# The down projection starts its seven-product blocks one quadruple earlier, loads one weight sum by itself, and moves some background sums

## The reference

```python
h = rms_norm(x, attn_norm);  p = h @ w_in            # 2048 -> 5376
mix = concat(sliding_window_attention(...), hgrn2(...))
x = x + mix @ w_out                                  # 2048 -> 2048
h = rms_norm(x, ffn_norm)
u = causal_conv3(h @ w_up) + conv_b                  # 2048 -> 2 x 5632
a, b = split(u)
x = x + (silu(a) * b) @ w_down                       # 5632 -> 2048
```

## Time and profile before

| | us |
|---|---|
| median of 3 runs | 1083.93 |
| the profiled execution | 1085.06 |
| its span | 1083.2 |
| PE busy | 1074.6 (99%) |
| DVE busy | 907.2 (84%) |
| ACT busy | 638.1 (59%) |
| POOL busy | 87.5 (8%) |

### The profile page before, as it was taken

The page is one execution under the profiler, slowest core; times in us unless marked ns, Lnnn a source line. Parts: engine busy times, 40 slices in busy tenths (PEclk is TensorE's granted clock), DMA queues, the critical chain, the costliest instruction groups (busy, mean ns, idle before and its releaser), DMA issues.

```text
span 1083.2 us, 18131 instructions
## 1 busy us (share of the span) xinstructions
PE 1074.6 (99%) x6537; PEld 925.9 (85%) x6537; DVE 907.2 (84%) x1342; ACT 638.1 (59%) x934; POOL 87.5 (8%) x130
## 2 busy tenths in 40 slices
PE   9999999999999999999999999999999999999998
PEld 8888888888888888888888888888888887787887
DVE  7888988979655578888888889888887888998998
ACT  7677675757445555555555555545554566657763
POOL 4500000000010010100100010001010000000000
PEclk9999999999999999999999999999999999999999
DMA  8656679787799988988988988989988689989794
GB/s 277 180 170 193 182 234 243 228 242 225 255 246 281 274 249 251 260 259 254 262 240 257 265 253 265 250 238 293 280 253 236 196 296 308 326 295 340 269 339 154
DMA packets 197008, 274.00 MB, mean 253 GB/s; under 512 B 9285, under 2 KB 144086, under 8 KB 196694
## 3 DMA queue, kind: packets, MB, share of 16 engines
q1 hardware_dynamic: 180758, 220.69, 62.4%
q0 software_dynamic: 12960, 47.19, 20.0%
q10 hardware_dynamic: 3232, 5.39, 1.3%
HBM read 267.86 MB, written 52.56 MB: 296 GB/s over the span
## 4 chain that ended last, share of the span: by engine, by line
PE 95%; DMA 3%; DVE 1%; issue 0%; ACT 0%; SPq 0%; DVEq 0%; ACTq 0%
PE bank L1828 38%; PE bank L1836 20%; PE bank L2221 6%; PE bank L2223 6%; PE bank L2222 6%; PE bank L2074 3%; PE bank L2075 3%; PE bank L2076 3%; PE bank L1875 2%; PE bank L1877 2%; PE bank L1876 2%; DMA slot<-u_sums 1%; PE bank L1796 1%; PE bank L1904 1%; DMA raw<-in_w_ffn_up_dram 1%; DMA xt<-in_x_dram 1%
## 5 line engine op out<-in xcount | busy, mean ns | idle before, releaser
L796 ACT CAST w_hi<-raw 128x1024 fp32r<-128x1024 f32 x299 | 312.3, 1049 | 245.9 <-PE bank L1836 107.3
L1209 DVE TENSOR_TENSOR w_lo<-raw,w_hi 128x1024 fp32r<-128x1024 f32 x299 | 364.0, 1222 | 107.2 <-ACT w_hi L796 106.5
L1828 PE MATMUL bank<-hs,w_hi 128*128 128x512 f32 x1792 | 423.0, 391 | 0.0
L1828 PEld LDWEIGHTS bank<-hs,w_hi 128*128 128x128 f32 x1792 | 331.2, 188 | 66.3 <-issue 0.9
L1836 PEld LDWEIGHTS bank<-hs,w_lo 128*128 128x128 f32 x1792 | 224.6, 191 | 5.7 <-issue 0.2
L1836 PE MATMUL bank<-hs,w_lo 128*128 128x256 f32 x1792 | 227.3, 283 | 0.0
L1175 ACT CAST hi_slot<-slot 128x1024 fp32r<-128x1024 f32 (+1 forms) x108 | 124.3, 1187 | 65.4 <-PE bank L2223 19.1
L1736 DVE TENSOR_TENSOR slot_lo<-slot,hi_slot 128x1536 fp32r<-128x1536 f32 (+1 forms) x74 | 142.1, 1957 | 3.6 <-ACT hi_slot L1175 2.4
L1654 DVE SCALAR_TENSOR_TENSOR C<-U,cols,C 128x256 f32<-128x256 f32 x176 | 73.4, 479 | 0.0
L2223 PE MATMUL bank<-hi_slot,gated 128*128 128x512 f32 (+1 forms) x186 | 72.0, 387 | 0.0
L2221 PE MATMUL bank<-hi_slot,gated 128*128 128x512 f32 (+1 forms) x186 | 72.0, 387 | 0.0
(11 more groups left out here) (249 smaller groups left out, 1191.2 us busy)
## 6 DMA issues: line engine op xcount, KB each, us to landing
raw<-in_w_ffn_up_dram SPq DMA_DIRECT2D x176, 512.0 KB, 5.7
u_sums<-in_w_ffn_down_dram POOLq DMA_DIRECT2D x62, 512.0 KB, 6.1
raw<-in_w_in_dram SPq DMA_DIRECT2D x51, 512.0 KB, 4.5
slot<-in_w_ffn_down_dram SPq DMA_DIRECT2D x40, 512.0 KB, 5.0
raw<-in_w_in_dram SPq DMA_DIRECT2D x66, 256.0 KB, 3.6
slot<-u_sums SPq DMA_DIRECT2D x22, 768.0 KB, 5.9
raw<-in_w_out_dram SPq DMA_DIRECT2D x32, 512.0 KB, 5.8
u_sums<-u_sums POOLq DMA_DIRECT2D x28, 512.0 KB, 7.2
```

What stands on the lines that cost most here:

```text
L796: act.copy(w_hi[:, i, :], raw[:, i, :]).then_inc(units_hi, 1)
L1209: dve.tensor_tensor(w_lo[:, i, :], raw[:, i, :], w_hi[:, i, :].bitcast(F32), ALU.subtract)\
L1828: m = pe.matmul(banks[b][:, :], w_hi[:, i, c], hs[:, 4 * i + k, :], start=(first and k == 0), stop=(final and k == 3))
```

## The change

- The first pair's pattern has three plain quadruples in the old ring in place of four, then eight sevens, a plain quadruple D in the small slot, nine sevens and a last plain one. The counts, 17 sevens and 5 plain ones, are as before. With three old quadruples the last up group splits six pieces, not eight, and which old piece frees which block is worked out by `last_old_in`.
- The fourth sum, where it lies in DRAM, has a load and a semaphore of its own; the two others are loaded when part y of the slot's last use is done.
- POOL's steps come every 8/3 units, not 14/5, and none waits for a unit from 110 to 119.

The diff, without the two `b_work` functions' inner lines (they skip the split of units 2 and 3 where a quadruple has only two) and the new semaphore's line:

```diff
@@ -79,7 +79,7 @@
 COLUMN_PAIRS = OUT_GROUPS // 2
-PATTERNS = ["CCCCSSSSSSSSSSSSSSSSSc", "CcSSSSSSSDSSSSSSSSSSCc"]
+PATTERNS = ["CCCSSSSSSSSDSSSSSSSSSc", "CcSSSSSSSDSSSSSSSSSSCc"]
 KINDS = "".join(PATTERNS)
@@ -94,7 +94,7 @@
 MERGE_BEHIND = [(22, "a"), (43, "b")]
-OLD_RING = 4
+OLD_RING = 3
 SLOTS = 4
@@ -114,8 +114,8 @@
 HI_SLOTS = 2
-SUM_STEP = (14, 5)
-FIRST_SUM_UNIT, SUM_PAUSE = 20, (30, 38)
+SUM_STEP = (8, 3)
+FIRST_SUM_UNIT, SUM_PAUSES = 20, [(30, 38), (110, 120)]
 SCRATCH = 1024
@@ -437,6 +438,10 @@
+        def fourth_sums_loaded(q):
+            n = sum(last_sum_in_dram(m) and SLOT_OF[m] == SLOT_OF[q] for m in range(OLD_RING, q + 1))
+            return 16 * n
+
         def piece_number(q, piece):
@@ -466,6 +471,10 @@
         LAST_OLD = part_number(OLD_RING - 1, "b")
+
+        def last_old_in(units):
+
+            return max(n for n in range(LAST_OLD - RING + 1, LAST_OLD + 1) if n % RING in units)
@@ -650,9 +659,9 @@
                 elif SLOT_OF[q] == 2:
-                    wait_until_used(sp, LAST_OLD - {"a": 3, "x": 2, "y": 1, "z": 1, "b": 1}[part])
+                    wait_until_used(sp, last_old_in({"a": (0, 1), "x": (0, 1), "y": (1, 2), "z": (2,), "b": (2, 3)}[part]))
                 elif SLOT_OF[q] == SMALL_SLOT and part == "b":
-                    wait_until_used(sp, LAST_OLD)
+                    wait_until_used(sp, last_old_in((3,)))
@@ -663,12 +672,12 @@
                 wait_for_slot(q, "y")
-                sums = 2
+                sp.dma_start(raw_blocks[:, 3:5, :],
+                             u_sums_v[n, 0:2, :, pair, :].rearrange("j p m -> p j m")).then_inc(others, 16)
                 if last_sum_in_dram(q):
                     wait_for_slot(q, "z")
-                    sums = 3
-                sp.dma_start(raw_blocks[:, 3:3 + sums, :],
-                             u_sums_v[n, 0:sums, :, pair, :].rearrange("j p m -> p j m")).then_inc(others, 16)
+                    sp.dma_start(raw_blocks[:, SUM_4_AT, :], u_sums_v[n, 2, :, pair, :])\
+                        .then_inc(fourth_loaded[SLOT_OF[q]], 16)
@@ -753,8 +762,9 @@
                 unit = FIRST_SUM_UNIT + step * SUM_STEP[0] // SUM_STEP[1]
-                if unit >= SUM_PAUSE[0]:
-                    unit += SUM_PAUSE[1] - SUM_PAUSE[0]
+                for first, end in SUM_PAUSES:
+                    if unit >= first:
+                        unit += end - first
                 pool.wait_ge(units_used, unit + RING)
@@ -1163,13 +1175,18 @@
                         act.wait_ge(sums_of_block_made, seven_of(pair, at) + 1)
+                        if last_sum_in_dram(q):
+                            act.wait_ge(fourth_loaded[SLOT_OF[q]], fourth_sums_loaded(q))
                     else:
                         wait_for_down(act, q, {"x": "a", "y": "b"}.get(part, part))
-                    if q == OLD_RING:
-                        act.wait_ge(units_split, {"x": LAST_OLD - 2, "y": LAST_OLD - 1, "z": LAST_OLD}[part] + 1 + RING)
-                    elif q == OLD_RING + 1:
-                        act.wait_ge(units_split, LAST_OLD + 1 + RING)
-                        wait_until_used(act, {"x": LAST_OLD - 3, "y": LAST_OLD - 2, "z": LAST_OLD - 1}[part])
+                    first_use = q < OLD_RING + HI_SLOTS
+                    if first_use and q % HI_SLOTS == 0:
+                        of_raw = last_old_in({"x": (0, 1), "y": (1, 2), "z": (2, 3)}[part])
+                        act.wait_ge(units_split, of_raw + 1 + RING)
+                    elif first_use:
+                        if part == "x":
+                            act.wait_ge(units_split, last_old_in((3,)) + 1 + RING)
+                        wait_until_used(act, last_old_in({"x": (0,), "y": (1,), "z": (2,)}[part]))
                     else:
@@ -1747,7 +1766,7 @@
                 elif SLOT_OF[q] == 2:
-                    wait_until_used(dve, LAST_OLD)
+                    wait_until_used(dve, last_old_in((2, 3)))
                 if not last_sum_in_dram(q):
```

More of the change, by code:

```diff
@@ L369, in hybrid_layer @@
         x2_parked, x2_back = sem("x2_parked"), sem("x2_back")
+        fourth_loaded = [sem(f"fourth_loaded{n}") for n in range(SMALL_SLOT)]
         down_loaded = {piece: [sem(f"down_loaded_{piece}{n}") for n in range(SLOTS)] for piece in "ab"}
@@ L1119, in a_work, with b_work @@
                     make_hi(quad, i)
-            def b_work(g, quad):
+            def b_work(g, quad, units=RING):
                 make_hi(quad, 0)
@@ L1124, in b_work @@
                 make_hi(quad, 1)
-                make_hi(quad, 2)
+                if units > 2:
+                    make_hi(quad, 2)
                 act.wait_ge(ab_made, g + 1 + FREE)
                 act.copy(gated[:, bass.ds(g * 2, 2), 0:SEQ], C[:, 1, :, :]).then_inc(gated_hi, 1)
-                make_hi(quad, 3)
+                if units > 3:
+                    make_hi(quad, 3)
             def hi_of_sums(g):
@@ L1157, in _ @@
             act.wait_ge(sum_parked, 16 * PARKED_SUMS)
-            b_work(UP_GROUPS - 1, Q_DOWN + 1)
+            b_work(UP_GROUPS - 1, Q_DOWN + 1, units=2 * OLD_RING - RING)
             def hi_of(pair, at):
@@ L1662, in a_work, with b_work @@
                     make_lo(quad, i)
-            def b_work(g, quad, sums_too=False):
+            def b_work(g, quad, sums_too=False, units=RING):
                 taps(g * 2 + 1, 1, g, quad)
@@ L1670, in b_work @@
                 dve.tensor_tensor(b, a, b, ALU.mult).then_inc(ab_made, 1)
-                make_lo(quad, 2)
+                if units > 2:
+                    make_lo(quad, 2)
                 dve.wait_ge(gated_hi, g + 1)
@@ L1677, in b_work @@
                     sums_of_activations(g)
-                make_lo(quad, 3)
+                if units > 3:
+                    make_lo(quad, 3)
             def sums_of_activations(g):
```

## The result

The changed kernel takes 1086.1 us (median of 20 runs, 1084.9 to 1087.25), the kernel before 1083.86 beside it (20 runs, 1081.44 to 1087.02): ratio 1.0023, interval 1.0017 to 1.0029. The change makes it 2.2 us slower; 1.5 faster was forecast.

The account below looks back on a forecast made before the run. PE was taken as the bound, busy 1074.6 of 1083.2 us, so only its pauses could change. Terms -1.5 + 2.7 + 0.4 + 0.5 - 2.3 - 1.3 = -1.5 us gave 1082.4 from the median 1083.93; range 1081.0 to 1084.8.

Parts of the forecast that it names:

- sums' pause: Change from output to up projection: no sum steps from about 353 to 378, faster weight loads, PE's pause shrinks; -1.5 us.
- Entry: First pair's first seven: high parts wait for PE's last old pieces, so it starts late and pauses again; +2.7 us.
- Parked burst: First pair's early sevens: the 1.18 MB fetch of parked sums sits before the fourth seven's loads, making them late; +0.5 us.
- Sevens without a lead: First pair's eight sevens after the old ring: DVE just keeps pace with PE, small losses; +0.4 us.
- Plain quadruple in the middle: First pair: DVE gains 3.0 us on PE, so the nine sevens behind lose nothing; -2.3 us.
- Fourth sum and second pair: Second pair's sevens: two sums load 1.36 us earlier, the fourth separately, so DVE starts sooner; -1.3 us.
- Rival B: Second pair's pause stays because the parked sums' burst sets when all bytes land; -0.3 for -1.3, 1083.4 us; chance 0.13.
- D: Rival: slow loads in the stretch without a lead, burst +3.2, second pair wins nothing; +2.5, 1086.4 us; chance 0.07.
- A: Rival: weight loads around 355 to 365 stay slow for other causes, first term falls away; 1083.9 us; chance 0.13.
- C: Rival: everything clears, the parked burst does not reach DVE; -2.9, 1081.0 us; chance 0.22.

Follow-up runs that it names:

- e8: The kernel before, profiled once more with no edit: 1083.95 us.
- e11: The kernel before, profiled a third time with no edit: 1082.87 us.
- e6: The changed kernel with the two hi slots exchanged, so that the first seven has hi slot 0: 1087.4 us, ratio 1.0032 to the kernel before.
- e5: The changed kernel with the first pair's parked sums fetched behind the second seven's loads, as in the kernel before: 1084.79 us, ratio 1.0015 to before.
- e2: The changed kernel with the old pattern, four old-ring quadruples and old sum steps, leaving the fourth sum's own load: 1081.61 us, ratio 0.998 to before.
- e10: The changed kernel with hi slots exchanged, both fetches of parked sums one quadruple earlier and the old sum steps: 1083.4 us, ratio 1.0001 to before.

## Why the prediction was wrong, point by point

The forecast was -1.5 us and +2.2 was measured, 3.7 apart. Two steps failed: the sums' pause was priced at 1.5 us that the kernel hardly pays, and the new pattern at +1.3 where the pairs of runs give +3.9 to +4.7, in the main because its burst was priced too low and its plain quadruple too high.

**The sums' pause, -1.5: the first step that failed.** The mechanism was read rightly: steps at 336.84, 345.68 and 379.68 for "near 336", "near 345" and "near 378", faster loads, the cast behind PE's last output unit, no gap. But the term was taken from one execution, which stood 1.2 us above its own median, and then subtracted from that median. The text put "how it stands to the median" as a scale (1.13 above) and did not ask which stall made it so. The two other traces of the same kernel answer that: they have no pause there, and start Down at 857.08 and 856.98 against 858.49. In the times the term is between -1.0 and +0.6, about nothing. Take the 1.5 us of the stall out of the trace of before, and the difference of the two traces is 2.5 us; the medians say 2.2. (The spans of e8 and e11, 1082.1 and 1081.0, are 2.1 and 3.2 under the changed kernel's 1084.2.) To stand above the median is not by itself a sign of this stall: over the changed kernel and the nine others with a median of their own, the profiled execution stood between 0.1 below and 3.2 above, 1.0 above on average.

**Entry, +2.7: right**, both in place and size (1.05 + 1.68), and e6 shows its cause: with hi slot 0, which waits for DVE only, both late starts go.

**Parked burst, +0.5: the second step that failed, its place right and its size not**: 1.66. The nearest row was the second pair's load (some 7.8 us in all), whose burst was issued 6 us ahead of it, with two weight loads in between. Here the same two weight loads stand between, but only 3.85 us lie between fetch and load (876.01 and 879.86), and the load took 9.12, the top of the bounds. e5 takes the burst away and with it the whole wait. A pause over 1 us there, with DVE waiting for `u_sums`, was one of the prediction's own signs of being wrong. This term and e6 also show what the sum left out: it added entry and burst as if they were independent. When the bytes land is set by the burst and by when PE's old pieces end, not by when the first sevens run. Shorten the entry alone, and PE waits longer for the same bytes.

**Sevens without a lead, +0.4:** the number is right (0.42), in part by luck. The 0.30 of it came right behind the burst's pause, and e5, which has no such pause, loses 0.08 + 0.12 = 0.20 there.

**Plain quadruple in the middle, -2.3:** measured -1.92, at its weak bound. The two last sevens of the pair lose 0.34 and 0.12 us, as they do in before (0.28 and 0.12) and in e2 (0.32 and 0.12): the lead did not take that part away. And the 2.3 to be won came from one execution again. Over the eight traces with the old pattern the first pair loses 1.8 us on average, so with 0.54 left the plain quadruple is worth some 1.3 us (an estimate), not 2.3.

**Fourth sum and second pair, -1.3:** -0.63 in the traces. The earlier, smaller load took as long as ever: from 990.03 the first arrivals took 7.81 us where 6.47 had been, and the earlier trace rows went from a median of 6.1 to 7.2. Rival B's reason, the full queue, was half right. A single trace misleads here too. The second pair lost 2.03 us in the profile of before, 2.57 and 2.08 in e8 and e11; it loses 1.40 in the changed kernel and 1.02 in e2. In e2, where nothing else changes, the term is 1.0 to 1.6, near the forecast, and e2's median is 1.8 under that of before; the traces do not say where the rest comes from. The Trainium skill's rule in "DMA: Bandwidth & Descriptors", section "Rules for kernel authors", to coalesce many small transfers, puts mostly overhead under 64 KB; the prediction stretched it to the 256 KB here, and by that reading the split wins nearly nothing. e2's ratio of 0.998 (0.997 to 0.999) decides against that reading for this split.

**The rivals.** D had the direction and nearly the time (1086.4 for 1086.1), by a burst term of +3.2 and nothing won in the second pair; the trace shows +1.66 and -0.63, and the rest of the way is the pause at 370 that was hardly there to be won. So its time is in part luck. It was to decide from a landing of 7.5 us on, and the fourth seven's was 9.12. A had the right number for the first term (nothing), for another reason: the loads did become fast. C is refuted by the fourth seven. The range, 1081.0 to 1084.8, reached to no case in which the first term was empty and the burst large: the two were held apart.

## What to carry to other kernels

Before a stall in a profile becomes a term of a forecast, set the profiled execution beside the kernel's median and profile the same kernel again: here it was 1.2 us above, and two more executions had no such stall. Where two waits stand one behind the other and the second is for bytes whose landing does not move with the first, they are not two terms; ask when those bytes land, counted from a fixed event. A burst moved to a few microseconds ahead of a load on a full queue can cost that load the burst's whole length: 1.18 MB are 3.1 us at the 377 GB/s of the window from 878 (an estimate), and the load took 4 us longer.

## What the runs showed of the hardware that I had not expected

**The clock after a wait of 2.3 or 3.2 us.** In e6 the fourth seven starts after 3.15 us of idle, and the matmuls from 895.06 to 898.05 are 0.43 us apart, not 0.23. In e10 the same follows 2.27 us of idle. The windows of e6, then of e10 (the columns are as in the earlier trace rows; PEclk is the third number from the end):

```profile
894.00:895.00 1.00, 1.00 (x6) 0.82 (x5) 1.00 (x1) 1.00 (x2) 0.00 (x0) 1.00 1.05 408
895.00:896.00 1.00, 1.00 (x4) 0.77 (x4) 1.00 (x2) 0.13 (x1) 0.00 (x0) 0.53 0.99 383
896.00:897.00 1.00, 1.00 (x4) 0.81 (x3) 0.97 (x2) 0.65 (x1) 0.00 (x0) 0.50 0.36 137
897.00:898.00 1.00, 1.00 (x3) 0.76 (x3) 1.00 (x1) 1.00 (x2) 0.00 (x0) 0.50 0.10 35
898.00:899.00 1.00, 1.00 (x5) 0.77 (x4) 1.00 (x2) 0.81 (x2) 0.00 (x0) 0.77 0.84 223
```

```profile
373.00:374.00 1.00, 1.00 (x5) 1.00 (x6) 1.00 (x1) 0.00 (x0) 0.00 (x0) 0.50 1.08 213
374.00:375.00 1.00, 1.00 (x6) 1.00 (x5) 0.07 (x1) 0.81 (x4) 0.00 (x0) 0.50 1.00 266
375.00:376.00 1.00, 1.00 (x3) 0.74 (x3) 0.64 (x3) 1.00 (x6) 0.00 (x0) 0.50 1.05 346
```

0.50 is the lower of the two levels, 1.2 of 2.4 GHz. The idle 1.47 us of the earlier trace rows and the 1.49 at 892.20 were followed by 1.00. In e6 the lower clock costs 8 matmuls 0.2 us each, 1.6 us on top of the wait; it sets in behind six matmuls at the full clock, in e10 at once. The Trainium skill, "TensorE: Matmul & The Clock Gate", section "What's actually happening", has the clock at one of two levels, set by how busy the array has been; these rows agree: 1.00 and 0.50, and values in between only where a window holds both.

**The same place, the same program, another stall.** The pause at 370 was 0 to 2.3 us in seven traces of kernels with the same work up to there. In e6 a pause of 1.0 us came in the up projection at 753.87, behind casts that had waited 3.21 us for a load, where no other trace has one. Here such differences from one execution to the next are as large as what the sums' pause or the fourth sum's own load is worth.
